# Down-projection weights in three places, another load order and another last pair in a hybrid layer's expert stage

## The reference, cut to what matters

```python
gu = xb @ w_gate_up[e] + b_gate_up[e]        # 1024 -> 2048: 8 MB of weights
gate, up = gu[:, :MOE_FF], gu[:, MOE_FF:]
gate = jnp.minimum(gate, SWIGLU_LIMIT)
up = jnp.clip(up, -SWIGLU_LIMIT, SWIGLU_LIMIT)
act = (up + 1.0) * (gate * jax.nn.sigmoid(SWIGLU_ALPHA * gate))
return act @ w_down[e] + b_down[e]           # 1024 -> 1024: 4 MB of weights
```

## Time and profile before

| | us |
|---|---|
| median of 3 runs | 1255.08 (1253.33 to 1256.19) |
| the profiled execution: its time | 1258.74 |
| its span, first to last instruction | 1256.7 |
| PE busy | 1152.5 (92%) |
| HBM read | 463.13 MB, 369 GB/s over the span |

### The profile page before, as it was taken

How to read it: one execution, slowest core, us unless ns; L and a number is a source line. 1 busy time by engine, 2 the same in 40 slices (tenths; PEclk the granted TensorE clock), 3 DMA queues, 4 the chain that set the end, 5 groups by cost and what they waited for, 6 DMA issues and landing times.

```text
span 1256.7 us, 14765 instructions
## 1 busy us (share of the span) xinstructions
PE 1152.5 (92%) x6083; PEld 601.5 (48%) x6083; DVE 322.5 (26%) x674; ACT 185.2 (15%) x316; POOL 106.0 (8%) x50
## 2 busy tenths in 40 slices
PE   4999999999999999998988989898999999999995
PEld 2999799778634434333333333333333333343431
DVE  1633554132232222212221212122121222222112
ACT  2475244100301000000000000000000010000001
POOL 0764343020000000000000000000000000000000
PEclk9999999999999999999999999999999999999998
DMA  9972763398789999999999999999999999999994
GB/s 350 340 231 90 231 217 101 102 414 371 291 363 424 428 428 429 429 428 428 429 428 428 430 427 429 430 427 429 429 428 430 428 428 421 386 429 429 428 426 176
DMA packets 62268, 464.67 MB, mean 370 GB/s; under 512 B 8437, under 2 KB 31098, under 8 KB 34586
## 3 DMA queue, kind: packets, MB, share of 16 engines
q1 hardware_dynamic: 60968, 462.13, 89.6%
q10 hardware_dynamic: 1218, 1.93, 0.5%
q0 software_dynamic: 48, 0.13, 0.0%
HBM read 463.13 MB, written 1.05 MB: 369 GB/s over the span
## 4 chain that ended last, share of the span: by engine, by line
PE 67%; DMA 26%; issue 3%; ACT 2%; DVE 1%; ACTq 0%; SPq 0%; DVEq 0%
PE ps L438 65%; DMA ring<-in_w_down_dram 22%; DMA ring<-in_w_gate_up_dram 3%; PE ps L871 1%; ACT kept L1195 1%; DMA ring<-in_w_in_dram 1%; DMA ring<-in_g_onorm_dram 1%; PE ps L893 0%; PE ps L446 0%; ACT w_hi L1003 0%; DVE ring L1662 0%; ACT ring L986 0%; DVE kept L1326 0%; ACT ring L1041 0%; ACT ring L1212 0%
## 5 line engine op out<-in xcount | busy, mean ns | idle before, releaser
L438 PE MATMUL ps<-ring,kept 128*64 128x512 f32 (+1 forms) x3280 | 713.7, 602 | 44.1 <-DMA ring<-in_w_down_dram 32.5
L438 PEld LDWEIGHTS ps<-ring,kept 128*64 128x64 f32 (+1 forms) x3280 | 230.9, 138 | 496.4 <-issue 428.7
L438 PE MATMUL ps<-kept 128*128 128x128 f32 (+5 forms) x744 | 139.2, 350 | 5.5 <-DVE kept L1564 1.6
L1191 ACT ACTIVATE kept<-kept 128x512 f32<-128x512 f32 x32 | 20.2, 630 | 746.3 <-DVE kept L1598 746.3
L1617 DVE TENSOR_TENSOR kept<-ps,kept 64x512 f32<-64x512 f32 x64 | 44.1, 689 | 315.9 <-PE ps L438 314.9
L438 PEld LDWEIGHTS ps<-kept 128*128 128x128 f32 (+2 forms) x744 | 94.1, 192 | 58.7 <-issue 53.2
L1598 DVE TENSOR_SCALAR kept<-ps 128x512 f32<-128x512 f32 x32 | 22.1, 691 | 371.2 <-PE ps L438 371.2
L1674 POOL TENSOR_TENSOR w_lo<-ring,w_hi 128x1024 fp32r<-128x1024 f32 x38 | 91.9, 2435 | 116.7 <-ACT w_hi L1003 116.7
L438 PE MATMUL ps<-ring 128*128 128x128 f32 (+4 forms) x560 | 87.1, 314 | 2.4 <-issue 2.4
L438 PEld LDWEIGHTS ps<-ring 128*128 128x128 f32 (+3 forms) x560 | 78.4, 193 | 11.0 <-issue 6.3
L438 PE MATMUL ps<-hT_hi,w_hi 128*128 128x256 f32 x272 | 78.4, 288 | 0.0
(11 more groups left out here) (227 smaller groups left out, 519.4 us busy)
## 6 DMA issues: line engine op xcount, KB each, us to landing
ring<-in_w_gate_up_dram SPq DMA_DIRECT2D x128, 2048.0 KB, 26.9
ring<-in_w_down_dram SPq DMA_DIRECT2D x63, 2048.0 KB, 23.8
ring<-in_w_ada_dram SPq DMA_DIRECT2D x24, 1024.0 KB, 5.4
ring<-in_w_in_dram SPq DMA_DIRECT2D x22, 1024.0 KB, 11.4
ring<-in_w_out_dram SPq DMA_DIRECT2D x4, 1024.0 KB, 15.7
ring<-in_w_o_fox_dram SPq DMA_DIRECT2D x2, 1024.0 KB, 9.8
ring<-in_w_o_delta_dram SPq DMA_DIRECT2D x2, 1024.0 KB, 12.2
kept<-in_w_down_dram SPq DMA_DIRECT2D x1, 2048.0 KB, 14.1
```

What stands on the lines that cost most here:

```text
L438: return pe.matmul(dst, lhsT, rhs, start=start, stop=stop, skip_group_check=True)
L1191: A(sig_a, gate_a, ACT.Sigmoid, scale=ALPHA).then_inc(S("sig_ready"), 1)
```

## The change

- The first halves of down weights have a place each for even experts (units 16, 17) and odd ones (the tile in `kept`, now `dn_kept`); the second halves of both keep units 18, 19. Each kind has a semaphore of its own.
- SP's order up to pair 9 is that in which PE frees the places (`by_place`); pair 10 (`TURN`) changes over, and pairs 11 to 14 are loaded in the order of use (`by_need`).
- In the first round the first refill (gate_up of expert 2, unit pair 0) is two loads of 1 MB, each issued when PE has used its own unit.
- The last pair (`last_by_need`, `last_pair`): both gate_ups are loaded and computed first, then down of the even expert, then down of the odd one. The last half of down weights goes to units 4, 5, which gate_up of the last even expert has left, in two loads of 1 MB with a semaphore each. The even expert's transposed activations get a tile apart (`act_t_last`), and DVE and ACT follow the order. PE waits for `y_moved` between the two downs.
- In the opening the transposes of the router weights move from after the first gate_up to ahead of its seventh k step.

```diff
+            def load_gu_row(e, par, u, k):
+                src = w_gate_up[0, e, u * 2 * P:(u + 1) * 2 * P, :].rearrange("(p k) n -> p k n", k=2)
+                s0 = par * KD + 2 * u
+                sp.dma_start(flat[:, (s0 + k) * UNIT:(s0 + k + 1) * UNIT], src[:, k, :]).then_inc(
+                    expert_chunk_sem(s0), 16)
...
+            def load_dn(e, par, j):
+                if j == 1:
+                    sp.dma_start(flat[:, 18 * UNIT:20 * UNIT], dn_rows(e, 1)).then_inc(S("dn_high_in"), 16)
+                elif par == 0:
+                    sp.dma_start(flat[:, 16 * UNIT:18 * UNIT], dn_rows(e, 0)).then_inc(S("dn_even_in"), 16)
+                else:
+                    sp.dma_start(dn_kept, dn_rows(e, 0)).then_inc(S("dn_odd_in"), 16)
...
-            def next_dn(I, i, par, js=range(2)):
-                for j in js:
-                    sp.wait_ge(S("dn_used"), I * 8 + (par * 4 - 4 + 2 * j + 2))
-                    load_dn(i * 2 + par, j)
+            def next_dn(I, i, par, j):
+                if j == 1:
+                    sp.wait_ge(S("dn_used"), I * 8 + par * 4)
+                else:
+                    sp.wait_ge(S("dn_used"), I * 8 + (par * 4 - 6))
+                load_dn(i * 2 + par, par, j)
+
+            def by_place(I, i, first_unit_whole=True):
+                if first_unit_whole:
+                    next_gu(I, i, 0)
+                else:
+                    for k in range(2):
+                        sp.wait_ge(S("gu_used"), I * 16 + (k - 15))
+                        load_gu_row(i * 2, 0, 0, k)
+                    next_gu(I, i, 0, range(1, 4))
+                next_dn(I, i, 0, 0)
+                next_dn(I - 1, i - 1, 1, 1)
+                next_gu(I, i, 1)
+                next_dn(I, i, 1, 0)
+                next_dn(I, i, 0, 1)
+
+            def by_need(I, i):
+                for par in range(2):
+                    next_gu(I, i, par)
+                    for j in range(2):
+                        next_dn(I, i, par, j)
+
+            def last_by_need(I, i):
+                for par in range(2):
+                    next_gu(I, i, par)
+                for j in range(2):
+                    next_dn(I, i, 0, j)
+                next_dn(I, i, 1, 0)
+                sp.wait_ge(S("gu_used"), I * 16 + 6)
+                rows = w_down[0, i * 2 + 1, 4 * P:8 * P, :].rearrange("(p k) n -> p k n", k=4)
+                for half, sem in enumerate((S("dn_last_in0"), S("dn_last_in1"))):
+                    at = 4 * UNIT + half * UNIT
+                    sp.dma_start(flat[:, at:at + UNIT].rearrange("p (k n) -> p k n", k=2),
+                                 rows[:, 2 * half:2 * half + 2, :]).then_inc(sem, 16)
...
-                if first:
-                    next_gu(I0 + 1, 1, 0)
-                    next_dn(I0, 0, 1, range(1, 2))
-                    next_gu(I0 + 1, 1, 1)
-                    next_dn(I0 + 1, 1, 0)
-                with sp.Fori(2 if first else 1, PAIRS - 3) as i:
-                    next_gu(I0 + i, i, 0)
-                    next_dn(I0 + (i - 1), i - 1, 1)
-                    next_gu(I0 + i, i, 1)
-                    next_dn(I0 + i, i, 0)
...
+                with sp.Fori(2 if first else 1, TURN) as i:
+                    by_place(I0 + i, i)
+                next_gu(I0 + TURN, TURN, 0)
+                next_dn(I0 + TURN, TURN, 0, 0)
+                next_dn(I0 + (TURN - 1), TURN - 1, 1, 1)
+                next_gu(I0 + TURN, TURN, 1, range(0, 2))
+                next_dn(I0 + TURN, TURN, 0, 1)
+                next_gu(I0 + TURN, TURN, 1, range(2, 4))
+                next_dn(I0 + TURN, TURN, 1, 0)
+                next_dn(I0 + TURN, TURN, 1, 1)
+                with sp.Fori(TURN + 1, PAIRS - 1) as i:
+                    by_need(I0 + i, i)
+                last_by_need(I0 + (PAIRS - 1), PAIRS - 1)
...
+            def last_pair(i, high, q):
+                gate_up(i, 0)
+                pe.wait_ge(S("y_moved"), i * 4)
+                scatter()
+                act_transposes(i, 0)
+                gate_up_bias(i, 1)
+                gate_up(i, 1)
+                pe.wait_ge(S("act_t_ready"), i * 2 + 1)
+                pe.wait_ge(S("gated_ready"), i + 1)
+                scat_transposes()
+                down(i, 0, high, range(1), act_t_last)
+                pe.wait_ge(S("scat_ready"), i + 1)
+                act_transposes(i, 1)
+                down(i, 0, high, range(1, 2), act_t_last)
+                pe.wait_ge(S("y_moved"), i * 4 + 2)
+                down(i, 1, high, last_of=q)
...
+            def last_experts(I, i):
+                activate(I, i, 0, False)
+                activate(I, i, 1, False)
+                take_scat(I)
+                move_y(I, 0)
+                move_y(I, 1)
```

More of the change, by code:

```diff
@@ L54, in layer_kernel @@
     PAIRS = E // 2
+    TURN = 10
     TOPK = 4
@@ L128, in layer_kernel @@
         assert o + 2793 + 1024 <= PERSIST
+        act_t_last = keep(o + 2281, 512)
         xtok = keep(0, 2048).rearrange("p (t d) -> p t d", t=TT)
@@ L397, in load_round @@
             def load_round(I0, first):
-                if not first:
+                if first:
+                    by_place(1, 1, first_unit_whole=False)
+                else:
+                    sp.wait_ge(S("dn_used"), I0 * 8)
                     next_gu(I0, 0, 0)
-                    next_dn(I0, 0, 0)
+                    next_dn(I0, 0, 0, 0)
+                    next_dn(I0, 0, 0, 1)
                     next_gu(I0, 0, 1)
-                if first:
-                    next_gu(I0 + 1, 1, 0)
-                    next_dn(I0, 0, 1, range(1, 2))
-                    next_gu(I0 + 1, 1, 1)
-                    next_dn(I0 + 1, 1, 0)
@@ L419, in load_round @@
[L419 to L423, removed]
+                    next_dn(I0, 0, 1, 0)
+                with sp.Fori(2 if first else 1, TURN) as i:
[3 more added lines that the diff above has]
+                next_dn(I0 + (TURN - 1), TURN - 1, 1, 1)
@@ L854, in gate_up_bias, with gate_up @@
                     mm(bank(4 + b), sel_r[:, par, :], bias_r[:, b, :], True, False)
-            def gate_up(i, par, first=False):
+            def gate_up(i, par, first=False, opening=False):
+                extra = 16 if par == 0 and not opening else 0
                 for k in range(KD):
@@ L872, in act_transposes, with down @@
                 last.then_inc(S("act_t_ps"), 1)
-            def down(i, par, early=False):
+            def down(i, par, high, js=range(2), acts=None, last_of=None):
                 e = i * 2 + par
-                pe.wait_ge(S("act_t_ready"), e + 1)
-                for k in range(KD):
+                acts = act_t if acts is None else acts
+                if js[0] == 0:
+                    pe.wait_ge(S("act_t_ready"), e + 1)
+                for k in range(4 * js[0], 4 * js[-1] + 4):
                     j, kk = k // 4, k % 4
[L879 to L884, removed]
+                    if kk == 0 and j == 0:
+                        pe.wait_ge(S("dn_odd_in" if par else "dn_even_in"), i * 16 + 16)
+                    if kk == 0 and j == 1 and last_of is None:
+                        pe.wait_ge(S("dn_high_in"), high + (par * 16 + 16))
+                    lhsT = acts[:, kk * P + j * 64:kk * P + j * 64 + 64]
+                    if j == 0:
+                        unit = dn_kept if par else flat[:, 16 * UNIT:18 * UNIT]
+                    elif last_of is None:
+                        unit = flat[:, 18 * UNIT:20 * UNIT]
+                    else:
+                        unit = flat[:, 4 * UNIT:6 * UNIT]
+                        if kk % 2 == 0:
+                            pe.wait_ge(S(f"dn_last_in{kk // 2}"), last_of * 16 + 16)
                     for d in range(2):
@@ L917, in _, with pair @@
             pe.wait_ge(S("bias_split"), 5)
-            def pair(i, first, more, opening=False):
-                gate_up(i, 0, first)
+            def pair(i, high, first, opening=False):
+                gate_up(i, 0, first, opening)
                 if opening:
@@ L927, in pair @@
                 gate_up_bias(i, 1)
-                down(i, 0)
+                down(i, 0, high)
                 pe.wait_ge(S("gated_ready"), i + 1)
@@ L1189, in expert @@
                 e = i * 2 + par
+                if par == 1 and not more:
+                    act.wait_ge(S("act_ready"), e)
                 act.wait_ge(S("gate_ready"), e + 1)
@@ L1194, in expert @@
                 act.wait_ge(S("act_t_ps"), e + 1)
-                A(act_t, bank(7), ACT.Copy).then_inc(S("act_t_ready"), 1)
+                A(act_t_last if par == 0 and not more else act_t, bank(7), ACT.Copy).then_inc(S("act_t_ready"), 1)
             def one_round(q):
@@ L1591, in take_xg, with activate @@
                 last.then_inc(S("xg_high_ready"), 1)
-            def expert(I, i, par, more):
+            def activate(I, i, par, more):
                 e = I * 2 + par
@@ L1637, in one_round @@
                 build(gated, 0, True).then_inc(S("gated_ready"), 1)
```

(5 more changed lines are left out.)

69 lines of the change are left out of this document (34 added, 35 removed).

## The result

| | before | changed |
|---|---|---|
| median, us | 1255.63 (4 runs, 1253.33 to 1256.63) | 1244.32 (4 runs, 1243.95 to 1246.25) |
| ratio to before | | 0.9916, 95% interval 0.9898 to 0.9933 |
| profiled execution: time / span | 1258.74 / 1256.7 | 1243.98 / 1242.1 |
| first gate_up starts | 333.89 | 329.34 |
| from there to the span's end | 922.8 | 912.8 |

What follows compares the result with a forecast made beforehand. DMA transfers were taken to bound the whole stage. Gaps closed (4.4 us) plus the last pair (5.8) made 10.2 us off the median 1255.08, so 1244.9 us; forecast 1242.5 to 1247.5, wider range 1241 to 1250.5.

Steps and rivals of the forecast that it cites:

- Transfers are the bound: Whole expert stage: DMA transfers set the pace at 4.895 us a load; PE has 4.9 us of slack per pair.
- The start: First refills up to the first down: gaps shrink from 7.2 to 2.35 us, 4.85 us gained.
- The loop: Pairs after the start: engines stay full, PE's waits move to about 3.6 and 1.3 us per pair; gain and cost nothing.
- The turn: Change-over at pair 10: a new gap of 3.5 us, or 5.2 if the clock falls once.
- the lead: Term in the turn's gap: the engines are 1.96 us ahead when PE starts the second half of down 19.
- no gain at the turn: Around pair 10: the old dent (0.5 + 3.1 us) goes and one of 3.5 us comes, so nothing is gained.
- The last pair: End of stage: last gate_up comes 9.8 us earlier, the chain after it costs 4.0 us more (18.4 against 14.4); 5.8 us gained.
- The sum: Whole span: 4.4 us from fewer gaps and 5.8 from the last pair, 10.2 us less than 1256.7.
- (a): Rival at the turn: no gap, because PE runs ahead; 3.5 us more gained, 1241.4 us; chance 0.12 with better.
- (d): Rival, slower: clock stays at half through the last pair, about 15 us late, 1260 us; chance 0.05.
- (b): Rival, smaller gain: clock falls in last pair and at turn, or a second gap opens behind it; 1248 to 1251 us; chance 0.19.
- (c): Rival: start's gain is paid back at turn and loop, last pair's chain takes its order's gain; 1254 us; chance 0.06.

Runs made afterwards that it cites:

- start_old: Changed kernel with the start as before: first refill whole, router transposes after the first gate_up, shared-place load first in pair 1; stage 917.3 us, ratio to before 0.9962.
- turn5: Changed kernel with the change-over at pair 5 instead of 10; stage 913.2 us, one run of 1243.92 us.
- whole_first: Changed kernel with its first refill in one load of 2 MB again; stage 912.6 us, one run of 1245.77 us.
- place_late: Changed kernel with, in pair 1, the load for the free even place waiting behind that for the shared place; stage 915.9 us, one run of 1251.95 us.
- last_whole: Changed kernel with the very last half of down weights in one 2 MB load instead of two of 1 MB; stage 914.4 us, one run of 1249.66 us.
- last_old: Changed kernel with the last pair loaded and computed as before, even expert whole, then odd; stage 919.0 us, ratio to before 0.9977.
- best_again: Repeat: changed kernel with more gate_up loads moved ahead of blocked down loads at the turn, first down refill in two 1 MB loads; stage 908.0 us, ratio to before 0.9886.

## Why the prediction was right, point by point

- **Transfers are the bound, and idle time of their engines is time.** Right. Gaps of 7.2 against 2.8 us at the start were worth 4.0 us (start_old); a full turn and a full down refill (4.3 to 5.2 and 1.3 us) were worth 4.2 to 5.3, somewhat less than they held. Start gaps compare only where the loads ahead of the stage had come equally far. turn5 has the changed kernel's start, 428 GB/s over its first 20 us and start gaps of 0.8 us in all, yet its stage took 913.2: it began with 0.7 MB more still to come (381.9 against 381.3 MB of weights after the first gate_up, summed over the trace's packets).
- **The start, 4.85 us forecast, 4.0 to 4.4 measured.** The size is right, the split is not. The prediction gave the refill by rows 1.6 us (0.75 + 0.25 for 2.6); whole_first shows it worth nothing measurable. This is the term that was mis-sized. The four loads of the first refill run out before the next place is free in either case, so an earlier start only moves idle time behind them. What counts is when the load after them flows: the third place (2.6 to 3.1 us, place_late) and, by difference and not run alone, PE's down, which starts 19.2 us after the first gate_up instead of 21.0. (A slip in its working, without effect: the 3.69 us to the first refill's issue are a quarter of the gate_up, 13.95/4, plus 0.2, not half of the work.)
- **The loop, nothing.** Right: five loads stay queued. The forecast waits of 3.6 and 1.3 us became one of 3.1 to 3.5 in four of six pairs. That the split loads cost nothing beyond their bytes also held: whole_first and last_whole each take one split out, and their stages are 912.6 and 914.4 us against the 912.8 to 913.7 with it.
- **The turn, 3.5 us forecast against 4.3 to 5.2.** The interval from PE's second half to SP's issue is 925.49 - 896.16 = 29.3 us (29.2 forecast), so what was too small is the rest of that sum. One part is the lead: 1.96 us holds only if PE is waiting, and in the changed kernel PE came late, as the clock had fallen at 866. That is not all of it. In place_late (below) and whole_first the clock had not fallen there, PE did wait for that half, 1.1 us, and the gap by the same 80 us is still 4.4 us (405 GB/s), while start_old, where it had fallen (5.25 us at 871.94), has 4.2. So in those two 0.9 us of excess came without a fall, and its cause stays open. The term "no gain at the turn" fits within 1 to 2 us: 3.6 us went and 4.3 to 5.2 came.

```profile
873.69 3.65 PE L492 MATMUL ps<-ring,kept 128*64 128x512 f32 x16 [2.04 <-DMA ring<-in_w_down_dram]
...
903.06 17.39 PE L492 MATMUL ps<-ring,kept 128*64 128x512 f32 x80 [1.12 <-DMA ring<-in_w_down_dram]
894.20:974.20 80.00, 75.13 (x353) 29.08 (x353) 15.18 (x35) 5.49 (x12) 0.00 (x0) 0.98 0.97 405
```

- **The last pair, 5.8 us.** last_old gave 5.7, the chain 18.4 us as forecast, and the clock stayed at 1.00. In last_old the half clock was 2.4 us of it; the 2.85 of the forecast are before's.
- **The sum.** 10.2 forecast, 10.0 between the two profiles' stages, 9.5 against the mean of three. The parts as measured, 4.0 + 5.7 - (0.7 to 1.6), make 8.1 to 9.0; the 0.5 to 1.4 us left are not explained, and before has one profile only. That the median of the first series met 1244.9 within 0.6 us is partly luck: the two later ones are 3 us higher and outside the range, and runs of one kernel differ by 6 us.
- **The rivals.** (a) and (d) are out: there was a gap, and no half clock in the last pair. (b) did not happen at the end, and no second gap opened behind the turn (427 GB/s or more in every slice from the 31st to the 39th); of it only a larger gap at the turn came true. (c), all paid back, is refuted by start_old.

## What to carry to other kernels

When transfers are the bound, write the stage as loads times the time of one, plus gaps, plus what follows the last data, and look only for the last two. A gap closed here only where the load after the queue's last one was issued earlier; starting the queue earlier moved it. Where an in-order issuer stands before one place, look in the list behind it for a load whose place is already free.

## What the runs showed of the hardware

The granted clock falls in unchanged code at places that differ from run to run. Ahead of the stage three stretches of 20 us differ most between the two profiles. If PE sets the pace there, an estimate from the clock column (the third last) is 20 x (0.09 + 0.07 + 0.07) = 4.6 us, as much as the 4.55 us between them; that PE does so is not shown. The first three rows are of before, then the same of the changed kernel:

```profile
20.00:40.00 20.00, 16.10 (x92) 9.94 (x91) 9.99 (x11) 9.93 (x12) 3.64 (x2) 0.91 1.04 342
80.00:100.00 20.00, 17.93 (x123) 17.40 (x122) 4.42 (x10) 16.69 (x22) 11.70 (x5) 0.84 0.42 152
240.00:260.00 20.00, 17.56 (x119) 10.37 (x119) 2.50 (x6) 4.56 (x20) 5.63 (x5) 0.93 0.78 277
```

```profile
20.00:40.00 20.00, 15.07 (x96) 9.33 (x95) 10.10 (x11) 9.83 (x12) 3.55 (x2) 1.00 1.04 340
80.00:100.00 20.00, 17.93 (x127) 17.40 (x127) 5.54 (x14) 15.33 (x21) 10.35 (x5) 0.91 0.37 130
240.00:260.00 20.00, 17.38 (x126) 10.31 (x126) 3.91 (x13) 4.56 (x20) 7.80 (x5) 1.00 0.95 340
```

In the stage, too, it fell without a wait for data: in the changed kernel the 16 matmuls at 430.28, 539.37 and 1000.10 took 5.3 us, behind nothing but the 1.5 us of the gather that every pair has, while the same place in other pairs took 3.65. Why there and not elsewhere stays open; no run was made for it. Second, loads of 1 MB in a full queue cost nothing beside those of 2 MB: best_again kept 430 GB/s over the stretch with its two smaller down loads (351.39 to 366.39).
